# Turning the feed-forward layers' hidden rows by VectorE and transfers inside SBUF instead of by TensorE

## The reference

```python
D_MODEL, SEQ, D_FF = 1024, 256, 2816

def swiglu(h, w_in, w_out):
    gu = h @ w_in
    return (jax.nn.silu(gu[..., :D_FF]) * gu[..., D_FF:]) @ w_out

x = x + FFN_RESIDUAL * rmsnorm(swiglu(rmsnorm(x, g[0]), w_in, w_out), g[1])
```

## Time and profile before

| what | value |
|---|---|
| runs | 1663.43, 1663.65, 1663.92 us, median 1663.65 |
| span of the profiled execution | 1660.0 us; the page gives no other time of its own for it |
| TensorE busy, clock granted | 1630.5 us (98%), 0.999 of full speed |
| VectorE, ScalarE busy | 1100.5 us (66%), 927.3 us (56%) |
| GpSimd busy | 165.8 us (10%) |
| queue of the weight loads | 293.86 MB, 50.2% of 16 engines' time |

### The profile page before, as it was taken

One profiled execution on the slowest core, in us unless ns is written; L12 is line 12 of the kernel. 1 busy time (PEld: TensorE's weight loads), 2 busy tenths in 40 slices (PEclk: granted clock), 3 DMA queues, 4 the chain that ended last, 5 costly groups with the idle time before them and its releaser, 6 DMA issues.

```text
span 1660.0 us, 22537 instructions
## 1 busy us (share of the span) xinstructions
PE 1630.5 (98%) x8990; PEld 1370.2 (83%) x8990; DVE 1100.5 (66%) x1567; ACT 927.3 (56%) x1559; POOL 165.8 (10%) x240
## 2 busy tenths in 40 slices
PE   9999999999999999999999999999999999999997
PEld 7888799788888877888878888788889889788886
DVE  5555667788877654969765556755567776655555
ACT  6555556655567585462465456645555444655555
POOL 0000001128301111900000000000000000000000
PEclk9999999999999999999999999999999999999999
DMA  6755443555555544441555555565544433555552
GB/s 239 259 199 197 171 165 127 185 196 184 195 187 189 212 169 152 177 179 52 199 179 190 187 183 188 190 223 196 180 175 178 144 112 127 184 203 178 197 184 102
DMA packets 50297, 295.93 MB, mean 178 GB/s; under 512 B 6072, under 2 KB 12688, under 8 KB 16528
## 3 DMA queue, kind: packets, MB, share of 16 engines
q1 hardware_dynamic: 49744, 293.86, 50.2%
q0 software_dynamic: 160, 0.52, 0.1%
q10 hardware_dynamic: 288, 0.11, 0.0%
HBM read 293.39 MB, written 1.09 MB: 177 GB/s over the span
## 4 chain that ended last, share of the span: by engine, by line
PE 88%; DVE 5%; ACT 4%; issue 1%; POOL 0%; DMA 0%; POOLq 0%; DVEq 0%; ACTq 0%
PE PS L2143 84%; PE PS L2365 2%; DVE wlo L1331 1%; PE PS L2288 1%; ACT SC L964 1%; ACT whi L747 1%; PE PS L2146 1%; PE PS L2580 0%; ACT wk L787 0%; DMA raw<-in_w 0%; DVE SC L1919 0%; DVE SC L1618 0%; DVE st L1602 0%; ACT wk L814 0%; DVE SC L1599 0%
## 5 line engine op out<-in xcount | busy, mean ns | idle before, releaser
L1337 DVE SCALAR_TENSOR_TENSOR wlo<-raw,ct,whi 128x512 fp32r<-128x512 f32 (+1 forms) x552 | 424.7, 814 | 258.4 <-ACT whi L751 258.3
L2143 PE MATMUL PS<-whi,xhi 128*128 128x512 f32 (+1 forms) x1312 | 505.6, 395 | 5.6 <-DVE wlo L1337 2.3
L751 ACT ACTIVATE whi<-raw,ct 128x512 fp32r<-128x512 f32 (+1 forms) x552 | 377.4, 734 | 225.8 <-PE PS L2143 169.1
L2143 PE MATMUL PS<-wlo,xhi 128*128 128x512 f32 (+1 forms) x1312 | 495.5, 387 | 0.0
L1331 DVE TENSOR_TENSOR wlo<-raw,whi 128x1024 fp32r<-128x1024 f32 x240 | 296.6, 1243 | 217.1 <-ACT whi L747 216.5
L2143 PE MATMUL PS<-whi,xlo 128*128 128x512 f32 (+1 forms) x1312 | 405.5, 387 | 0.0
L747 ACT ACTIVATE whi<-raw 128x1024 fp32r<-128x1024 f32 x240 | 251.7, 1057 | 259.1 <-PE PS L2143 192.7
L2143 PEld LDWEIGHTS PS<-whi,xhi 128*128 128x128 f32 x1312 | 246.0, 188 | 60.0 <-DVE wlo L1331 4.2
L2143 PEld LDWEIGHTS PS<-whi,xlo 128*128 128x128 f32 x1312 | 246.4, 188 | 51.3
L2143 PEld LDWEIGHTS PS<-wlo,xhi 128*128 128x128 f32 x1312 | 246.7, 188 | 47.5
L2143 PE MATMUL PS<-whi,hhi 128*128 128x512 f32 x544 | 173.3, 392 | 0.1
(11 more groups left out here) (282 smaller groups left out, 1503.5 us busy)
## 6 DMA issues: line engine op xcount, KB each, us to landing
raw<-in_w SPq DMA_DIRECT2D x263, 1024.0 KB, 4.8
gr<-in_rows SPq DMA_DIRECT2D x14, 512.0 KB, 3.8
SC<-scratch SPq DMA_DIRECT2D x5, 512.0 KB, 5.8
X<-in_x SPq DMA_DIRECT2D x2, 512.0 KB, 5.2
raw<-in_w SPq DMA_DIRECT2D x2, 512.0 KB, 6.9
SC<-scratch SPq DMA_DIRECT2D x4, 256.0 KB, 5.2
xn<-in_sc SPq DMA_DIRECT2D x2, 512.0 KB, 6.4
SC<-scratch SPq DMA_DIRECT2D x1, 1024.0 KB, 7.5
```

What stands on the lines that cost most here:

```text
L751: e = a.activation(hi[:, f], src[:, f], ACT.Copy, scale=ct[:, c:c + 1])
L1337: e = v.scalar_tensor_tensor(lo[:, f], src[:, f], ct[:, c:c + 1], hi[:, f].bitcast(f32), MUL, SUB)
L2143: return pe.matmul(o, l, r, start=start, stop=stop)
```

## The change

In the chunks 1 to 9 of each layer (`is_moved`), 54 in all, TensorE doesn't turn the hidden rows any more. VectorE writes the hidden product in an order of 32-channel blocks into `hb`, and one `transpose` turns all 32x32 blocks of that 128x512 tile at once, into `tb` (where `sg` was). A block is then turned in itself, but lies in the wrong 32 partitions; sixteen transfers of 32 partitions x 512 bytes, issued by SP, bring each to its own partitions in `hb`. Four of them (shift 0) keep the partitions. ScalarE and VectorE then read the high and low part from `hb`, in SBUF, instead of from PSUM. The columns of the up weights of these chunks are put in another order on the host, so that blocks and channels match. Chunks 0 and 10 stay as they were. With a unit being two half units and `up_at(n, j) // 2` the first unit of chunk j, SP issues the first four moves behind the load of unit +4 (the second up unit of chunk j + 1) and the other twelve behind the load of unit +5 (the down unit of chunk j).

```diff
+N_MOVED = NJ - 2
+def moved(n, j):
+    return N_MOVED * n + j - 1
+def is_moved(j):
+    return 0 < j < NJ - 1
+MOVES = {}
+for n in range(6):
+    for j in range(1, NJ - 1):
+        MOVES[up_at(n, j) // 2 + 4] = (moved(n, j), (0,))
+        MOVES[up_at(n, j) // 2 + 5] = (moved(n, j), (1, 2, 3))
...
+        tb, hb = wk[:, 0:2 * S], wk[:, 2 * S:4 * S]
...
+        def by_block(a):
+            return a.rearrange("p (q c) -> p q c", c=32)
+        def hidden_in_blocks(h):
+            return hb.rearrange("p (q h c) -> p q h c", q=8, h=2)[:, :, h, :]
+        def hidden_by_token(n, j):
+            if not is_moved(j):
+                return PS[:, turn_bank(n), :].rearrange("p (i t) -> p i t", i=2)
+            return hb.rearrange("p (a q c) -> p q a c", a=4, q=4)
+        def in_tokens(a, j):
+            return a.rearrange("p i (h a c) -> p (i h) a c", h=2, a=4) if is_moved(j) else a
...
                     sp.dma_start(raw[:, u % NRAW, :], w[u]).then_inc(s_raw[u % NRAW], 16)
+                    if u in MOVES:
+                        m, shifts = MOVES[u]
+                        q.wait_ge(s_tb, m + 1)
+                        for i in shifts:
+                            for t in range(4):
+                                f = (t + i) % 4
+                                sp.dma_start(hb[32 * f:32 * f + 32, 128 * t:128 * t + 128], tb[32 * t:32 * t + 32, 128 * f:128 * f + 128]).then_inc(l_hb, 16)
...
                 def hidden_hi(j):
-                    J = NJ * n + j
-                    q.wait_ge(s_hT, J + 1)
+                    if is_moved(j):
+                        q.wait_ge(l_hb, 256 * moved(n, j) + 256)
+                    else:
+                        q.wait_ge(s_hT, 2 * n + 1 + (j > 0))
...
-                    p = PS[:, turn_bank(n), :].rearrange("p (i t) -> p i t", i=2)
-                    a.activation(hhi[:, 2 * (j % 2):2 * (j % 2) + 2, :], p, ACT.Copy).then_inc(s_hhi, 1)
+                    d = hhi[:, 2 * (j % 2):2 * (j % 2) + 2, :]
+                    a.activation(in_tokens(d, j), hidden_by_token(n, j), ACT.Copy).then_inc(s_hhi, 1)
...
                 def hidden(j, h):
...
-                    if j:
-                        q.wait_ge(s_hT, J)
-                    v.scalar_tensor_tensor(hf[:, h, :], PS[:, up_bank(n, j) + h, S:2 * S], r2[k][h], sg[:, h, :], MUL, MUL).then_inc(s_hm, 1)
+                    if j == 1:
+                        q.wait_ge(s_hT, 2 * n + 1)
+                    elif j:
+                        q.wait_ge(s_hlo, J)
+                    up = PS[:, up_bank(n, j) + h, S:2 * S]
+                    if not is_moved(j):
+                        v.scalar_tensor_tensor(hf[:, h, :], up, r2[k][h], sg[:, h, :], MUL, MUL).then_inc(s_hm, 1)
+                        return
+                    v.scalar_tensor_tensor(hidden_in_blocks(h), by_block(up), r2[k][h], by_block(sg[:, h, :]), MUL, MUL).then_inc(s_hm, 1)
+                    if h:
+                        q.wait_ge(s_hm, 2 * J + 2)
+                        v.transpose(tb, hb).then_inc(s_tb, 1)
...
                 def hidden_lo(j):
...
+                    if is_moved(j):
+                        q.wait_ge(l_hb, 256 * moved(n, j) + 256)
+                    v.tensor_tensor(in_tokens(hlo[:, f, :], j), hidden_by_token(n, j), in_tokens(hhi[:, f, :].bitcast(f32), j), SUB).then_inc(s_hlo, 1)
...
-                        if j and tiles[0] == 1:
-                            hidden_turned(j - 1)
+                        if j == 1 and tiles[0] == 1:
+                            hidden_turned(0)
...
+            gate, up = (w_in[:, at:at + 256] for at in (256 * j, FF + 256 * j))
+            if is_moved(j):
+                gate, up = (m.reshape(D, 2, 4, 32).transpose(0, 2, 1, 3).reshape(D, 256) for m in (gate, up))
+            rows_(np.concatenate([gate, up], 1), 512)
```

More of the change, by code:

```diff
@@ L272, in program @@
         s_gu, s_silu, s_hm, s_hT, s_hhi, s_hlo = (sem(n) for n in ("s_gu", "s_silu", "s_hm", "s_hT", "s_hhi", "s_hlo"))
+        s_tb, l_hb = sem("s_tb"), sem("l_hb")
         s_sq, s_yg, s_ms, s_r1, s_X, s_r2, s_xn = (sem(n) for n in ("s_sq", "s_yg", "s_ms", "s_r1", "s_X", "s_r2", "s_xn"))
@@ L1512, in hidden @@
                     q.wait_ge(s_silu, 2 * J + h + 1)
-                    if j:
-                        q.wait_ge(s_hT, J)
-                    v.scalar_tensor_tensor(hf[:, h, :], PS[:, up_bank(n, j) + h, S:2 * S], r2[k][h], sg[:, h, :], MUL, MUL).then_inc(s_hm, 1)
+                    if j == 1:
[10 more added lines that the diff above has]
+                        v.transpose(tb, hb).then_inc(s_tb, 1)
                 def hidden_lo(j):
                     q.wait_ge(s_hhi, NJ * n + j + 1)
-                    p = PS[:, turn_bank(n), :].rearrange("p (i t) -> p i t", i=2)
                     f = slice(2 * (j % 2), 2 * (j % 2) + 2)
-                    v.tensor_tensor(hlo[:, f, :], p, hhi[:, f, :].bitcast(f32), SUB).then_inc(s_hlo, 1)
+                    if is_moved(j):
+                        q.wait_ge(l_hb, 256 * moved(n, j) + 256)
+                    v.tensor_tensor(in_tokens(hlo[:, f, :], j), hidden_by_token(n, j), in_tokens(hhi[:, f, :].bitcast(f32), j), SUB).then_inc(s_hlo, 1)
                 for j in range(NJ):
@@ L2990, in ffn @@
         for j in range(NF // 2):
-            rows_(np.concatenate([w_in[:, 256 * j:256 * j + 256], w_in[:, FF + 256 * j:FF + 256 * j + 256]], 1), 512)
+            gate, up = (w_in[:, at:at + 256] for at in (256 * j, FF + 256 * j))
+            if is_moved(j):
+                gate, up = (m.reshape(D, 2, 4, 32).transpose(0, 2, 1, 3).reshape(D, 256) for m in (gate, up))
+            rows_(np.concatenate([gate, up], 1), 512)
             if j:
```

## The result

The changed kernel takes 1858.51 us (median of 1856.6 to 1860.05) beside 1663.79 us for the one before: ratio 1.117, 95% interval 1.1157 to 1.1183, slower by 194.7 us. The forecast was 1643.5 us, faster, with a range of 1637 to 1657.

What follows compares the result with a forecast made beforehand. TensorE, busy 98% of the span, was taken to bound the kernel. 26.1 us for the turns less 6 us for tight layers gave 20.1 us: 1663.65 - 20.1 = 1643.5 us, range 1637 to 1657.

Steps and rivals of the forecast that it cites:

- TensorE's share: Four turns gone from each of 54 moved chunks, taken as 0.48 us a chunk: 26.1 us off TensorE's chain.
- VectorE's and ScalarE's share: Transpose of 0.70 us a chunk on VectorE; ScalarE's high part from 582 to about 628 ns; low part costed at nothing.
- The tight layers: Second and third layers: low part late 0.75 us in 8 of 18 chunks, 6 us; rival 1655.5 us, chance 0.22.
- SP's queue: Sixteen issues a chunk on SP at 0.48 us; load +6 goes 1.9 us late, covered by waits for raw data.
- The price of an issue: One move's issue on SP, taken as 0.48 us from four issues in 1.93 us; low end 0.33.
- The slower rival: SP's twelve issues make the low part late above 0.70 us each; at 0.80 the kernel takes 1703 us; chance 0.10.
- The fixed cost: About 2.0 us on each transfer; paid in turn, twelve would take 24 us; the trace has them overlap.

Runs made afterwards that it cites:

- e1: The changed kernel without the sixteen moves of each chunk, high and low parts waiting for VectorE's transpose alone; 1646.1 us.
- e6: The changed kernel with only the first, fourth, fifth, sixth layers moved; SP issues six moves, GpSimd six and copies four blocks; 1651.9 us, ratio 0.9928.
- e8: As e6, but GpSimd issues all twelve moves and SP none; 1658.8 us, ratio 0.9969 to the kernel before.
- e2: The changed kernel with each of the sixteen moves carrying 16 of its 128 columns, issues unchanged in number and place; 1854.5 us.
- e4: The changed kernel with four blocks copied by ScalarE and twelve moves split 3, 6, 3 over loads +4, +5, +6; 1718.4 us, ratio 1.0325.

## Why the prediction was wrong, point by point

**TensorE's share: right.** A moved chunk costs 16.33 instead of 16.80 us where nothing is late (e1, e6, e8).

**VectorE's and ScalarE's share: right.** The transpose takes 711 ns (0.70 taken), the high part 629 ns (628), the low part 693 ns.

**The tight layers: right in kind and nearly in size.** 6 us were taken for them, 8.3 us are lost in e1, in those two layers; in fewer and longer waits than the 8 of 0.75 us that were forecast (6, of up to 2.8 us).

**SP's queue: the step that failed**, as the prediction put it: "load +6, now at 95.33, goes at 97.2, 1.9 us late. The waits for raw data cover this: ScalarE works several units ahead". I followed one chunk only, and took a delay that comes back in every chunk as one that is covered once. The units that ScalarE works ahead are the reason for the opposite: the split of load +6's weights stands ahead of silu and hidden product in program order, so the next transpose waits for load +6, and the next moves and loads wait for that transpose. (The chain shows this order; no run with less splitting ahead tests it.) The runs show a period of 20.0 us in place of 16.3, and without the moves (e1) 16.3 and 1646.1 us. Going round once at my own price, 16 x 0.48 = 7.7, with 0.6 + 5.05 + 4.4 from the changed kernel, is 17.7 us, over 16.8; with the load's issue and landing as the kernel before has them (0.33 and, by its page, 4.8 us) it is 17.2. So with the circle seen the estimate would have been 1686 to 1664 + 54 x 0.9 = 1713 us, slower. By the changed kernel's terms the limit lies at 16x = 16.8 - 10.05, x = 0.42 us for an issue.

**The price of an issue: mis-sized.** 0.63 us, not 0.48. 16 x 0.15 x 54 = 130 us more, the larger part of the distance from 1713 to 1858.5 us; the rest is in periods above 20.0, the most of it in the first two layers.

**The slower rival: right engine, wrong wait.** It had SP's twelve issues decide, but through the moves' landing against TensorE's need, with a limit of 0.70 to 0.74 us. At 0.63 us, and with the last move landing after 1.8 us, that rival doesn't bind, and the kernel is slower all the same, because load +6 behind the moves binds first. Its 1703 us were the wrong sum for another reason.

**The fixed cost, rightly not summed.** The Trainium skill (DMA: Bandwidth & Descriptors, "Anatomy of one DMA") puts a fixed cost of about 2.0 us on a transfer, for those that GpSimd issues; that it might be paid in turn was the prediction's own thought. It isn't: a move lands after 1.7 us or more, and the next is issued 0.63 us behind it. But something is paid in turn, the 0.63 us on the issuing queue, and the rows of before show four such issues in a row and not sixteen.

## What to carry to other kernels

When a change puts work into an in-order queue, don't ask whether one delay is covered; follow the dependencies on until they come back to the same instruction of the next iteration, and compare the sum of that circle with the bound engine's period. Look at what is prepared ahead: here it stands early in program order, and that closed the circle. Count small transfers by issues, not by bytes, ask what large transfer stands in front of them, and look for an issuing queue that has nothing else in it.

## What the runs showed of the hardware that was not expected

- A move of 32 partitions costs SP 0.63 us whether it carries 16 KB or 2 KB (e2), and the weight load issued right behind one 0.58 us instead of 0.33. Why it is more than the 0.48 us of the four parameter loads wasn't tried.
- GpSimd issues the same move in 0.50 us, from a queue of its own, but pauses: 2.3, 5.8 and 6.3 us in 432 issues (e8), 3.0 us in 216 (e6). The cause of the pauses is open.
- A move behind a 1 MB load lands after 3.8 to 4.6 us instead of 1.8 (e4 and the changed kernel). A queue of its own doesn't spare it: of GpSimd's six moves in e6 the four ahead of SP's load +5 land after 1.7 us, the two behind it after 5.0, and in e8, with twelve, the median is 3.6 us.
- TensorE, idle for 4.6 us, came back at half clock (0.50 granted) for about 5 us: 12 products in 5.0 us instead of 2.72 (first layer of the changed kernel).
